# Loading the projection weights without waiting for x, and the output bias row before the first norm

## The chip, the cores and the metric

One Trainium2 chip, one core. The metric is the device time of one launch in microseconds (us). The kernel before takes 1614.23 us (median of 3 runs, 1613.65 to 1616.16). All intermediate work is float32, with matrix products done as three products of float32r (a reduced-precision float32 form for the tensor engine) high and low parts.

## The reference

One encoder layer on 512 tokens of width 1024: RMSNorm, a mixer (a gated depthwise convolution beside a neighbourhood attention, both fed by one input projection), a residual, RMSNorm, a top-4-of-32 mixture of experts, a residual and a last RMSNorm.

```python
def mixer(xn, w_in, b_in, conv_w, conv_b, ln_g, ln_b, rpb, w_out, b_out):
    proj = jnp.einsum("bsd,de->bse", xn, w_in) + b_in          # 1024 -> 2560
    glu_a, glu_g, q, k, v = jnp.split(proj, [...], axis=-1)    # five parts of 512
    conv_out = conformer_conv(glu_a, glu_g, conv_w, conv_b, ln_g, ln_b)   # 31 taps
    na_out = neighbourhood_attention(q, k, v, rpb)
    mixed = jnp.concatenate([conv_out, na_out], axis=-1)
    return jnp.einsum("bse,ed->bsd", mixed, w_out) + b_out

def reference(x, ...):
    h = x
    h = h + mixer(rmsnorm(h, g_mix[0]), ...)
    h = h + moe(rmsnorm(h, g_ffn[0]), ...)      # 32 experts, 3 matrices of 1024 x 1024 each
    return rmsnorm(h, g_final)
```

## The kernel before

Each engine has its own program, written out by hand; semaphores alone order them. There is no planner: what stands in the code is the order of each engine.

Stage 1, the first norm. The 512 tokens are four tiles of 128. SP issues four transfers of x, one per tile, into `h` (L400), then the two small ones of `b_in` and `conv_w` (L401, L402) into a staging area. ACT issues the row of `g_mix`, spread to all partitions (L641), and three small vectors (L644). For each tile ACT squares it and sums (L663), POOL computes 1/rms in two short operations (L514, L516), and DVE scales the tile into `xn_tile` (L939; both inputs, `h` and the `g_mix` row, lie in SBUF). PE turns the tile in eight transposes (L1306); behind those of tile 0 it also turns the staged columns (L1311, L1313), for which it waits for all five small transfers. ACT and DVE copy the turned tile out of PSUM as its high part (L649, L944), and DVE subtracts to get the low part (L949, one input in PSUM).

Stage 2, the input projection. `w_in` comes as five blocks of 512 columns, 2 MB each, into five units of `ring`; SP issues them in the order 1, 0, 2, 3, 4 (L408). Ahead of that SP waits until all four x tiles have landed (L405, L406). A block is used in four groups of 128 columns (the last one in row groups). For each group ACT makes the high part (L677), and the low part is made by DVE for groups 0 to 7 (L961) and by POOL for 8 to 19 (L530); the subtraction reads two SBUF operands. PE runs 24 matmuls per group (L1320, L1321, L1322). Group g needs its low part and a free PSUM bank.

Between the two, POOL adds the row `b_out`, again spread to all partitions (`bout_row`), to each tile of `h` (L525). It waits for that row's transfer, and for tile n until DVE has made `xn_tile` of it (`xn_ready`). ACT issues that transfer (L666) after its last copy of stage 1. The sum is used only much later.

Stage 3. The gate (L969) writes the convolution's input, and the 31 taps run on DVE alone (L978, L986, 4 x 31 instructions). POOL meanwhile builds the attention's bias tables (L544), whose raw rows SP loads pair by pair of heads (L428), each pair after the tables of the one before. Behind these loads on SP stand the two transfers of `w_out` (L433, L435). Then come layer norm of the convolution, attention, output projection, routing and the 32 experts, whose weights stream through SP's queue.

Behind the `w_in` loads SP also issues an 8 MB write of zeros to `y_rows` (L412) and the 16 copies of the position bias (L418).

Of the kernel before, what the change touches and what calls it, by code (L numbers as in the profile page):

```python
# [15 lines left out]
SEQ, D_MODEL = 512, 1024  # L16
GRID_W, N_ROWS = 64, 8
QB = 16
NQ = GRID_W // QB
# [37 lines left out]
def encoder_kernel(nc, x, g_mix, w_in, b_in, conv_w, conv_b, ln_g, ln_b, rpb, w_out, b_out,  # L57
# [3 lines left out]
    with ctx:  # L61
        def sem(name):
            return ctx.enter_context(nc.semaphore(name))
# [52 lines left out]
        def unit(s):  # L116
            return ring[:, s, :].rearrange("p (k f) -> p k f", k=KD)
# [39 lines left out]
        bout_row = area_k[:, 1024:2048]  # L157
# [87 lines left out]
        x_loaded = [sem(f"x_loaded{n}") for n in range(NQ)]  # L245
# [4 lines left out]
        bout_loaded = sem("bout_loaded")  # L250
# [109 lines left out]
        def row_bcast(ap, n, offset=0):  # L360
            return bass.AP(ap.tensor, ap.offset + offset, [[0, P], [1, n]])
# [9 lines left out]
        def piece_src(i, e):  # L371
            return w_rows[i // 4][e, :, (i % 4) * PIECE:(i % 4 + 1) * PIECE]
# [24 lines left out]
        @block.sync  # L397
        def _(sp):
            for n in range(NQ):
                sp.dma_start(h[:, n, :], x_blocks[n]).then_inc(x_loaded[n], 16)  # L400
            sp.dma_start(stage[0:20, 0, :], b_in[0].rearrange("(c p) -> c p", p=P)).then_inc(stage_loaded, 16)  # L401
            sp.dma_start(stage[0:CONV_K * CC, 1, :],  # L402
                         conv_w[0].rearrange("k (c p) -> (k c) p", p=P)).then_inc(stage_loaded, 16)

            for n in range(NQ):  # L405
                sp.wait_ge(x_loaded[n], 16)  # L406
            for i, col in enumerate((1, 0, 2, 3, 4)):
                sp.dma_start(unit(1 + i), win_v[:, :, col * HALF:(col + 1) * HALF]).then_inc(win_loaded[i], 16)  # L408

            spare = y_rows[N_EXPERTS * CAP:, :].rearrange("(p i) (j f) -> p (i j) f", p=CAP, f=HALF)  # L410
            sp.wait_ge(zeros_ready, 1)
            sp.dma_start(spare, zeros[0:CAP].unsqueeze(1).to_broadcast([CAP, spare.shape[1], spare.shape[2]])).then_inc(y_stored, 16)  # L412

            sp.wait_ge(rpb_tile_loaded, 16)
            for c in range(QB):
                sp.dma_start(rpb_pad[c], rpb_tile[:, :]).then_inc(rpb_stored, 16)  # L418
            sp.wait_ge(rpb_stored, 16 * QB)
            copy_size = (HEADS * RPB_H + 1) * RPB_PITCH  # L420
            for pair in range(HEADS // 2):
                if pair:
                    sp.wait_ge(tables_ready, 6 * pair)
                for r in range(N_ROWS):
                    start = (2 * pair * RPB_H + WIN_H - 1 - r) * RPB_PITCH + QB - 1
                    src = bass.AP(rpb_pad.tensor, rpb_pad.offset + start,
                                  [[copy_size - 1, QB], [RPB_H * RPB_PITCH, 2], [1, RUN]])
                    sp.dma_start(raw_bias[r * QB:(r + 1) * QB, :, :], src).then_inc(raw_loaded, 16)  # L428
            def load(i, e):
                sp.dma_start(w_raw[i][:, :], piece_src(i, e)).then_inc(raw_piece[i], 16)  # L430

            sp.wait_ge(proj_done, 12)
            sp.dma_start(unit(1), wout_v[:, :, HALF:]).then_inc(wout_loaded[1], 16)  # L433
            sp.wait_ge(proj_done, 20)
            sp.dma_start(unit(6), wout_v[:, :, 0:HALF]).then_inc(wout_loaded[0], 16)  # L435
            for i in range(3):
                load(i, 0)
            sp.wait_ge(wout_done, 2 * NQ)
            for i in (3, 4):
                load(i, 0)  # L440
            sp.wait_ge(xn2_stored, 16 * NQ)
            load(5, 0)
            load(6, 0)
            sp.wait_ge(bias_rows_loaded, 128)
            for i in range(7, 10):
                load(i, 0)
            sp.wait_ge(overflow_ready, 2)
            sp.wait_ge(xg_loaded, 16)
            load(10, 0)
            sp.wait_ge(xn2_transposed, 2 * NQ)  # L450
            load(11, 0)

            def reload(i, e, at):
                sp.wait_ge(piece_used, at + 1)
                load(i, e)

            for i in range(GATE, DOWN):
                reload(i, 1, i)
            with sp.Fori(0, N_EXPERTS - 2) as j:
                for i in range(DOWN):  # L460
                    reload(i, j + 2, PIECES * j + 8 + i)
                for i in range(DOWN, PIECES):
                    reload(i, j + 1, PIECES * j + 8 + i)
            for i in range(DOWN, PIECES):
                reload(i, N_EXPERTS - 1, PIECES * (N_EXPERTS - 2) + 8 + i)
            trips = sp.value_load(n_ovf[0:1, 0:1], min_val=0, max_val=MAX_OVERFLOW)
            with sp.If(trips > 0):
                with sp.Fori(0, trips) as t:
                    e = sp.value_load(ovf_exp[0:1, bass.ds(t, 1)], min_val=0, max_val=N_EXPERTS - 1)
                    for i in range(PIECES):  # L470
                        reload(i, e, EXTRA_BASE - PIECES + PIECES * t + i)
            for n in range(NQ):
                sp.wait_ge(final_ready, n + 1)
                sp.dma_start(out_blocks[n], y_tok[:, n * TOP_K, :]).then_inc(out_stored, 16)
            sp.wait_ge(out_stored, 16 * NQ)
# [163 lines left out]
        def _(act):  # L639
# [3 lines left out]
            for i, vec in enumerate((conv_b, ln_g, ln_b)):  # L643
                act.dma_start(stage[20 + CC * i:20 + CC * (i + 1), 0, :],  # L644
                              vec[0].rearrange("(c p) -> c p", p=P)).then_inc(stage_loaded, 16)
            def xnT_half(n):

                act.wait_ge(xn_transposed, 2 * n + 2)
                s.copy(xnT_high[:, 4:8, n * P:(n + 1) * P],  # L649
                       bank[4 + (2 * n + 1) % 4][:, :].rearrange("p (k t) -> p k t", k=4)).then_inc(xnT_act, 1)  # L650
# [12 lines left out]
                s.activation(junk_norm[n % 2], h[:, n, :], ACT.Square, accum_out=ss[:, n:n + 1]).then_inc(ss_ready, 1)  # L663
            for n in range(NQ):
                xnT_half(n)
            act.dma_start(bout_row, row_bcast(b_out, D_MODEL)).then_inc(bout_loaded, 16)  # L666
            def win_high_part(g):
                loaded, high, _ = split_parts(g)
                act.wait_ge(win_loaded[4 if g >= 16 else groups[g][0] - 1], 16)

                if 4 <= g < 8:
                    act.wait_ge(proj_done, g - 3)
                elif 9 <= g < 16:
                    act.wait_ge(proj_done, 8)
                elif g >= 16:
                    act.wait_ge(proj_done, 12)
                s.copy(high, loaded).then_inc(win_high_ready, 1)  # L677
# [52 lines left out]
            for i in range(NS):  # L730
                n, hd = steps[i]
# [562 lines left out]
        def _(pe):  # L1294
# [30 lines left out]
            for g in range(16):  # L1325
                if g < 8:
                    pe.wait_ge(win_low_dve, g + 1)
                else:
                    pe.wait_ge(win_low_pool, g - 7)

                if 4 <= g < 12 and g % 2:
                    pe.wait_ge(glu_ready, 4 * ((g - 4) // 2 + 1))
                elif 4 <= g < 12:
                    pe.wait_ge(act_evac, (g - 4) // 2 + 1)
                elif g >= 12:
                    pe.wait_ge(act_evac, 4 + g - 12 + 1)
                _, high, low = split_parts(g)
                for k in range(KD):
                    last = three_products(bank[g % 4][:, :], high[:, k, :], low[:, k, :], xnT_high[:, k, :], xnT_low[:, k, :], k)
                last.then_inc(proj_done, 1)  # L1340
# [245 lines left out]
```

## Time and profile before

| | before |
|---|---|
| median of 3 runs | 1614.23 us |
| profiled execution, its own time | 1613.65 us |
| span of that execution's trace | 1611.9 us |
| PE busy | 1438.2 us (89%) |
| DVE busy | 1293.6 us (80%) |
| ACT busy | 951.7 us (59%) |
| POOL busy | 272.7 us (17%) |
| DMA moved | 476.44 MB, mean 296 GB/s |

The span is cut into engines' busy time; a busy share is an average over stages. The 32 experts fill about the last 1280 us, and PE is busy there nearly throughout. The change lies in the first 60 us, so the rows below are mostly of that stretch. Start times are in us from the start of the span. A matmul's end is modelled, and spans on POOL are rough; the distance between starts is more to be trusted there.

### The profile page before, as it was taken

The page shows a single profiled execution, that of the slowest core. Times are in us where ns is not written, and L with a number is a line of the kernel's source. Part 1 is how long each engine was busy: PE and PEld are TensorE (multiplying, and loading weights), DVE is VectorE, ACT ScalarE, POOL GpSimd, SP SyncE. Part 2 cuts the span into 40 slices and gives each one's busy share as a digit, 9 for nine tenths or more (in the row PEclk, how much of TensorE's full clock was granted, in tenths as well). Part 3 has the DMA queues.
Part 4 walks back from the last instruction along what each step waited for, and adds up shares of the span by engine and source line. Part 5 has one row for each costly group of instructions (what it writes and reads, how often), then busy time and mean ns, then how long its engine had stood idle before and what let it go on. Part 6 is the DMA issues. An engine that isn't in the chain of part 4 may idle for free.

```text
span 1611.9 us, 19217 instructions
## 1 busy us (share of the span) xinstructions
PE 1438.2 (89%) x6488; PEld 1094.5 (68%) x6488; DVE 1293.6 (80%) x933; ACT 951.7 (59%) x708; POOL 272.7 (17%) x287
## 2 busy tenths in 40 slices
PE   4995389956999999999999999999999999999950
PEld 3884157744777777777777777777777777777730
DVE  6899444275888888888888888888888888888836
ACT  2230153233677777777777777777777777777621
POOL 3297730041000000000000000000000000000004
PEclk9998569966999999999999999999999999999985
DMA  7800400075899999999999999999999999999436
GB/s 248 314 10 26 178 17 1 30 261 184 320 363 371 381 376 374 371 376 367 372 370 373 374 374 376 376 373 375 363 371 366 365 395 375 370 373 377 154 140 244
DMA packets 84049, 476.44 MB, mean 296 GB/s; under 512 B 10716, under 2 KB 11015, under 8 KB 34871
## 3 DMA queue, kind: packets, MB, share of 16 engines
q1 hardware_dynamic: 71518, 432.48, 70.5%
q0 software_dynamic: 6560, 23.55, 4.4%
q10 hardware_dynamic: 5944, 20.08, 3.3%
q8 instruction: 15, 0.25, 0.1%
q14 instruction: 12, 0.09, 0.0%
HBM read 448.44 MB, written 27.63 MB: 295 GB/s over the span
## 4 chain that ended last, share of the span: by engine, by line
PE 83%; POOL 5%; DVE 5%; DMA 3%; ACT 1%; issue 1%; SPq 1%; POOLq 0%; DVEq 0%; ACTq 0%
PE pair L1498 22%; PE pair L1497 22%; PE pair L1496 22%; PE pair L1503 3%; POOL area_t L544 3%; PE pair L1320 2%; PE pair L1321 2%; PE pair L1322 2%; PE pair L1476 2%; PE pair L1483 1%; DVE h L1284 1%; PE pair L1362 1%; DMA area_m<-in_conv_w 1%; PE pair L1381 1%; POOL ring L544 1%
## 5 line engine op out<-in xcount | busy, mean ns | idle before, releaser
L1124 DVE TENSOR_TENSOR w_low<-w_raw,w_high 128x2048 fp32r<-128x2048 f32 x381 | 867.3, 2291 | 142.5 <-ACT w_high L794 142.4
L794 ACT CAST w_high<-w_raw 128x2048 fp32r<-128x2048 f32 x384 | 734.2, 1913 | 323.3 <-PE pair L1498 314.9
L1498 PE MATMUL pair<-w_high,xT_low 128*112 128x512 f32 x1024 | 405.2, 396 | 0.0
L1496 PE MATMUL pair<-w_high,xT_high 128*112 128x512 f32 x1024 | 404.9, 395 | 0.0
L1497 PE MATMUL pair<-w_low,xT_high 128*112 128x512 f32 x1024 | 404.9, 395 | 0.0
L1497 PEld LDWEIGHTS pair<-w_low,xT_high 128*112 128x112 f32 x1024 | 179.6, 175 | 58.1
L1496 PEld LDWEIGHTS pair<-w_high,xT_high 128*112 128x112 f32 x1024 | 179.8, 176 | 57.3
L1498 PEld LDWEIGHTS pair<-w_high,xT_low 128*112 128x112 f32 x1024 | 179.5, 175 | 57.0
L1496 PE MATMUL pair<-w_high,hT_high 128*112 128x512 f32 x512 | 202.3, 395 | 0.0
L1498 PE MATMUL pair<-w_high,hT_low 128*112 128x512 f32 x512 | 202.2, 395 | 0.0
L1497 PE MATMUL pair<-w_low,hT_high 128*112 128x512 f32 x512 | 201.3, 393 | 0.0
L591 POOL CAST sel_gate<-is_expert 128x112 fp32r (+1 forms) x32 | 32.5, 1014 | 656.7 <-PE pair L1498 656.7
L1497 PEld LDWEIGHTS pair<-w_low,hT_high 128*112 128x112 f32 x512 | 89.6, 175 | 30.1
L1498 PEld LDWEIGHTS pair<-w_high,hT_low 128*112 128x112 f32 x512 | 89.6, 175 | 29.4
L1496 PEld LDWEIGHTS pair<-w_high,hT_high 128*112 128x112 f32 x512 | 89.3, 174 | 28.7
L986 DVE SCALAR_TENSOR_TENSOR area_m<-area_u,convT,area_m 128x512 f32<-128x512 f32 x120 | 108.0, 976 | 0.0
L595 POOL CAST sel_down<-is_expert 128x112 fp32r (+1 forms) x32 | 9.2, 287 | 366.3 <-PE pair L1498 366.3
L1232 DVE SCALAR_TENSOR_TENSOR area_q<-area_t,area_q 112x1024 f32<-112x1024 f32 x32 | 65.3, 2041 | 0.0
L737 ACT ACTIVATE area_a<-area_a,area_u 128x256 f32<-128x256 f32 (+1 forms) x32 | 18.0, 561 | 57.6 <-DVE area_u L1023 57.6
L1322 PE MATMUL pair<-xnT_high,win_low 128*128 128x512 f32 x128 | 50.8, 397 | 0.0
L544 POOL TENSOR_TENSOR area_t<-area_m 128x384 f32<-128x384 f32 x8 | 46.5, 5808 | 16.2 <-DMA area_m<-rpb_pad 16.2
L843 ACT CAST xT_high<-pair 128x896 fp32r<-128x896 f32 x33 | 29.6, 898 | 25.9 <-PE pair L1476 25.9
(246 smaller groups left out, 1422.4 us busy)
## 6 DMA issues: line engine op xcount, KB each, us to landing
w_raw<-in_w_gate SPq DMA_DIRECT2D x128, 1024.0 KB, 6.9
w_raw<-in_w_up SPq DMA_DIRECT2D x128, 1024.0 KB, 6.7
w_raw<-in_w_down SPq DMA_DIRECT2D x128, 1024.0 KB, 6.8
y_rows<-area_m ACTq DMA_DIRECT2D x32, 448.0 KB, 5.5
ring<-in_w_in SPq DMA_DIRECT2D x5, 2048.0 KB, 19.1
y_rows<-area_t SPq DMA_DIRECT2D x1, 8064.0 KB, 37.7
ring<-in_w_out SPq DMA_DIRECT2D x2, 2048.0 KB, 10.4
h<-in_x SPq DMA_DIRECT2D x4, 512.0 KB
```

Source lines behind the costliest of these rows:

```text
L544: g.tensor_tensor(dst.rearrange("p (m r c) -> p m r c", r=N_ROWS, c=QB), src, mask[:, o:o + w].rearrange("p (m r c) -> p m r c", r=N_ROWS, ...
L591: g.tensor_copy(sel_gate[:, :], is_expert[:, bass.ds(e, 1)].to_broadcast([P, CAP]))
L794: s.copy(w_high[:, i % HIGH_RING, :], w_raw[i][:, :]).then_inc(high_ready, 1)
L986: v.scalar_tensor_tensor(mixedT[:, c, :], u_pad[:, c, bass.ds(k, SEQ)], convT[:, bass.ds(k * CC + c, 1)], mixedT[:, c, :], ALU.mult, ALU.a ...
L1124: v.tensor_tensor(w_low[i][:, :], w_raw[i][:, :], w_high[:, i % HIGH_RING, :].bitcast(F32), ALU.subtract).then_inc(low_ready, 1)
L1232: v.scalar_tensor_tensor(h_tok.rearrange("q (k p) -> q p k", k=KD), g_silu.rearrange("q (p k) -> q p k", k=KD), SILU_TOP, u_lim.rearrange( ...
L1320: t.matmul(to, a_high, b_high, start=(k == 0), stop=False)
L1322: return t.matmul(to, a_low, b_high, start=False, stop=(k == KD - 1))
L1496: t.matmul(to[half], tok_high, hi, start=False, stop=False)
L1497: t.matmul(to[half], tok_high, lo, start=False, stop=False)
L1498: last = t.matmul(to[half], tok_low, hi, start=False, stop=(k == KD - 1))
L1503: t.matmul(to[half], sel[:, :], rows[:, half * HALF:(half + 1) * HALF], start=True, stop=False)
```

## The change

Two edits. SP no longer waits for the four x tiles before it issues the five loads of `w_in`. And the transfer of the `b_out` row, which ACT issued after its four copies of the first norm, is issued directly behind the three small vectors, before the first square.

```diff
@@ SP
             sp.dma_start(stage[0:CONV_K * CC, 1, :],
                          conv_w[0].rearrange("k (c p) -> (k c) p", p=P)).then_inc(stage_loaded, 16)
 
-            for n in range(NQ):
-                sp.wait_ge(x_loaded[n], 16)
             for i, col in enumerate((1, 0, 2, 3, 4)):
                 sp.dma_start(unit(1 + i), win_v[:, :, col * HALF:(col + 1) * HALF]).then_inc(win_loaded[i], 16)
@@ ACT
             for i, vec in enumerate((conv_b, ln_g, ln_b)):
                 act.dma_start(stage[20 + CC * i:20 + CC * (i + 1), 0, :],
                               vec[0].rearrange("(c p) -> c p", p=P)).then_inc(stage_loaded, 16)
+            act.dma_start(bout_row, row_bcast(b_out, D_MODEL)).then_inc(bout_loaded, 16)
+
@@
             for n in range(NQ):
                 xnT_half(n)
-            act.dma_start(bout_row, row_bcast(b_out, D_MODEL)).then_inc(bout_loaded, 16)
```

On ACT the order of the first instructions was this (area_k holds the two rows, area_t takes the squares, xnT_high is the high part of the turned tile, glu_high that of the weights):

```order
L644 DMA area_m<-in_conv_b 4x128
L644 DMA area_m<-in_ln_g 4x128
L644 DMA area_m<-in_ln_b 4x128
L663 ACT_TABLE_LOAD
L663 ACTIVATE area_t,ss<-h 128x1024 [waits x_loaded0]
L663 ACTIVATE area_t,ss<-h 128x1024 [waits ss_ready,x_loaded1]
L663 ACTIVATE area_t,ss<-h 128x1024 [waits ss_ready,x_loaded2]
L663 ACTIVATE area_t,ss<-h 128x1024 [waits ss_ready,x_loaded3]
L649 CAST xnT_high<-pair 128x4x128 [waits xn_transposed] x4
L666 DMA area_k<-in_b_out 128x1024
L677 CAST glu_high<-ring 128x1024 [waits win_loaded0]
```

In the changed kernel it is this:

```order
L642 DMA area_m<-in_conv_b 4x128
L642 DMA area_m<-in_ln_g 4x128
L642 DMA area_m<-in_ln_b 4x128
L644 DMA area_k<-in_b_out 128x1024
L663 ACT_TABLE_LOAD
L663 ACTIVATE area_t,ss<-h 128x1024 [waits x_loaded0]
L663 ACTIVATE area_t,ss<-h 128x1024 [waits ss_ready,x_loaded1]
L663 ACTIVATE area_t,ss<-h 128x1024 [waits ss_ready,x_loaded2]
L663 ACTIVATE area_t,ss<-h 128x1024 [waits ss_ready,x_loaded3]
L649 CAST xnT_high<-pair 128x4x128 [waits xn_transposed] x4
L676 CAST glu_high<-ring 128x1024 [waits win_loaded0]
```

One DMA instruction moved past the squares and the copies. On SP no instruction moved, only the waits on x are gone; PE, DVE and POOL have the same instructions in the same order.

## Rows read from the trace of the kernel before

**Rows 1.** Chain of waits, 0 to 60 us: start us, us, what.
```profile
5.08 15.30 DMA area_m<-in_conv_w
...
21.14 0.87 PE pair L1306 x4
22.01 1.28 DVE area_q L939
...
30.73 1.14 DVE win_low L961
32.01 0.77 PE pair L1320
...
37.47 0.42 PE pair L1320
37.88 0.23 PE pair L1321
```

**Rows 2.** Chain of waits, 140 to 230 us.
```profile
142.76 33.12 POOL area_t L544
...
183.18 7.91 DMA ring<-in_w_out
```

**Rows 3.** Who waits, PE, 32 to 141 us: us in total, times, longest.
```profile
PE pair L1320 <- DVE win_low L961: 3.6, 1, 3.6
```

**Rows 4.** Timeline of DVE: start us, us, line, operation, count [idle before, releaser].
```profile
22.00 1.28 DVE L939 SCALAR_TENSOR_TENSOR area_q<-h,rstd,area_k 128x1024 f32<-128x1024 f32 x1
23.20 0.68 DVE L944 CAST xnT_high<-pair 128x512 fp32r<-128x512 f32 x1
...
25.12 1.28 DVE L939 SCALAR_TENSOR_TENSOR area_q<-h,rstd,area_k 128x1024 f32<-128x1024 f32 x1
...
30.64 1.22 DVE L961 TENSOR_TENSOR win_low<-ring,glu_high 128x1024 fp32r<-128x1024 f32 x1
35.48 10.13 DVE L961 TENSOR_TENSOR win_low<-ring,glu_high 128x1024 fp32r<-128x1024 f32 x3 [3.62 <-ACT glu_high L677]
45.96 1.13 DVE L969 SCALAR_TENSOR_TENSOR area_u<-pair,colT,area_v 128x128 f32<-128x128 f32 x4 [0.34 <-PE pair L1322]
...
56.78 1.13 DVE L969 SCALAR_TENSOR_TENSOR area_u<-pair,colT,area_v 128x128 f32<-128x128 f32 x4 [6.68 <-PE pair L1322]
```

**Rows 5.** Timeline of POOL, 20 to 66 us.
```profile
21.25 0.55 POOL L516 TENSOR_TENSOR rstd<-ms,small 128x1 f32<-128x1 f32 x1
35.47 12.42 POOL L525 TENSOR_TENSOR h<-h,area_k 128x1024 f32<-128x1024 f32 x4 [13.66 <-DMA area_k<-in_b_out]
```

**Rows 6.** POOL's additions at L525: duration ns min/median/max, first and last start.
```profile
L525 POOL TENSOR_TENSOR h<-h,area_k x4: 2383/3385/3392, 35.5 to 44.5; 128x1024 f32<-128x1024 f32 x4
```

**Rows 7.** Timeline of ACT, 0 to 40 us.
```profile
3.24 1.28 ACT L663 ACT_TABLE_LOAD   x1 [3.24 <-issue]
9.31 1.06 ACT L663 ACTIVATE area_t<-h 128x1024 f32<-128x1024 f32 x1 [4.79 <-DMA h<-in_x]
...
19.74 1.06 ACT L663 ACTIVATE area_t<-h 128x1024 f32<-128x1024 f32 x1 [2.14 <-DMA h<-in_x]
...
28.94 1.05 ACT L677 CAST glu_high<-ring 128x1024 fp32r<-128x1024 f32 x1
34.40 2.94 ACT L677 CAST glu_high<-ring 128x1024 fp32r<-128x1024 f32 x3 [4.42 <-DMA ring<-in_w_in]
```

**Rows 8.** DMA queues, 0 to 6 us: packets, MB, share of 16 engines.
```profile
q10 hardware_dynamic: 152, 0.53, 38.2%
```

**Rows 9.** DMA queues, 10 to 18 us.
```profile
q1 hardware_dynamic: 323, 1.22, 50.4%
```

**Rows 10.** DMA queues, 28 to 36 us.
```profile
q1 hardware_dynamic: 1288, 2.61, 88.2%
q10 hardware_dynamic: 144, 0.52, 16.8%
```

**Rows 11.** Timeline of SP, 0 to 31 us.
```profile
5.08 0.27 SPq L402 DMA_DIRECT2D area_m<-in_conv_w  x1
19.80 16.52 SPq L408 DMA_DIRECT2D ring<-in_w_in  x5
```

**Rows 12.** Busy time by stretch: PE, PEld, DVE, ACT, POOL (instructions), clock, DMA share, GB/s.
```profile
60.00:131.00 71.00, 71.00 (x315) 58.80 (x314) 71.00 (x72) 17.98 (x22) 45.67 (x19) 1.00 0.26 82
```

## The prediction

> **What bounds the kernel now.** I read the chain of waits first, for the stretch that the change touches. It begins with the x transfers' queue: the small transfer of `conv_w` is issued at 5.08 and lands at 20.38, then come PE's transposes, then DVE work without a break, and PE's first projection matmul starts at 32.01 [rows 1]. Next I read who PE waits for between 32 and 141 us: only that one wait of 3.6 us, for DVE's first low part, and none after it [rows 3]. So from 32.01 on the projection is PE at its own pace. DVE, in turn, idles 6.68 us for PE ahead of the gate at 56.78 [rows 4], and is then busy for the whole of 60 to 131 us [rows 12]. POOL's table at 142.76 ends only when the taps do, and the `w_out` load at 183.18 hangs behind it [rows 2]. Hence the reader is to see one chain: PE's first projection matmul, group 3 of the projection, the gate, the taps, the tables, `w_out`, and everything behind. There is no slack on it between 32 us and the end, so a shift of PE's start is a shift of the end, microsecond for microsecond. The whole question is when that first matmul starts.
>
> What does it wait for? The first weight block does not appear: ACT takes its group 0 at 28.94 without waiting for a transfer. ACT waits 4.42 us for the second block, until 34.40 [rows 7]. The low part of group 1 is made from 35.48 and is ready about 3.4 us later, near 38.9 (three such operations take 10.13 us) [rows 4]. PE needs it after the 24 matmuls of group 0: about 13 of 0.43 us and 11 of 0.23 us from 32.01 [rows 1], so near 40.2. It is there 1.3 us early. So neither weight block is late for PE now.
>
> **SP's removed wait.** SP could issue `w_in` at 5.4 instead of 19.8 [rows 11]. What it buys is small. While x runs, queue 1 keeps 50.4% of 16 engines busy [rows 9], which I read as eight engines full and eight idle: 323 packets in 8 us x 16 x 0.504 = 64.5 us of engine time are 0.20 us for a 4 KB packet, no slower per byte than the 2 KB packets of the weights (8 x 16 x 0.882 = 113 us over 1288, 0.088 us each) [rows 10]. On the eight idle engines the weights' halves start early; on the eight that carry x they stand behind x in the same queue and end when they end now, plus what x is late. So the first block still lands around 28 to 30 us, and PE did not wait for it. Value 0. Its bounds: at best, if a weight wait were hidden in PE's slow start, the 13 matmuls would run at 0.23 instead of 0.43 us, a gain of 2.6 us; at worst the loads take packets from x (rival 3).
>
> The Trainium skill (page "DMA: Bandwidth & Descriptors", section "Why a DMA increments its semaphore by 16 and not by 1", and its summary row on using all 16 engines) has a copy run on as many engines as its slowest dimension allows; the x tile's slowest source dimension is 8 grid rows. The 50.4% agrees with eight.
>
> **The moved `b_out` transfer, on the queue.** 128 rows of 4 KB, 0.52 MB, on ACT's queue 10, and all 16 engines take part. Now it runs in 28 to 36 us beside the weights; there it costs nothing that PE waits for. In the changed kernel it follows `g_mix` directly and runs into x. Its issue (0.4 us or so) is before the table load at 3.24 and ACT idles 4.79 us before x lands at 9.31 [rows 7], so ACT loses nothing. But each of the eight full engines must also carry eight of its packets. Their price: in 0 to 6 us queue 10, which is `g_mix`, took 38.2% of 6 us, 2.3 us per engine, or (6 x 16 x 0.382)/152 = 0.24 us a packet, 1.9 us for eight [rows 8]. In 28 to 36 us queue 10 took 16.8% of 8 us, 1.3 us per engine [rows 10]. I take 1.9, the row of the same stage beside the same x transfers; bounds 1.3 and 2.3, and 0 if the engines have gaps (rival 2). Since x is back to back (landings at about 9.3 and 19.7 [rows 7]), all of it lands later by that, `conv_w` behind it too, and with both the chain of rows 1. **+1.9 us.**
>
> **The moved `b_out` transfer, on POOL.** POOL's four additions waited for this row until 35.47 [rows 5], when DVE's urgent part was over. Now the row is there early, and POOL starts as soon as its last 1/rms is done: 21.25 + 0.55 = 21.80 in the old times. That is the middle of the DVE run 22.00 to 31.9 that starts PE. The trace shows what they do to each other: three low parts that take 1.22 us alone took 10.13 us beside the additions, 3.4 each [rows 4], and an addition takes 3.39 beside them [rows 6], so they take turns; less DVE's 1.15 an addition holds for 2.2 us. The gate at 45.96, which reads PSUM and one SBUF operand, took the same 1.13 us beside POOL as at 56.78 without it [rows 4]. So of DVE's run only the operations with two SBUF inputs are hit: tile scalings 2 and 3 (L939) and the first low part (L961).
>
> The Trainium skill ("SBUF — State Buffer", on the port pair that DVE and GpSimd share) says the pair is an exclusive lock for a whole instruction, taken by DVE when both of its inputs are in SBUF; it would make the scaling wait like the subtraction. The 3.4 us agree for the subtraction; no row shows the scaling beside POOL.
>
> Played through in the old times (add 1.9 to all): addition 0 from 21.80 to 24.0. Scaling 2 wanted 22.00, gets 24.0: 2.0 late. Addition 1 from 25.2 to 27.4. Scaling 3 comes 3.12 us after scaling 2 (22.00 to 25.12), so wants 27.1, gets 27.4: 2.3 late. Addition 2 from 28.6 to 30.8, addition 3 to 33.0. The low part comes 5.52 us after scaling 3 (25.12 to 30.64), wants 32.9, gets 33.0: 2.4 late. **+2.4 us** on PE's start. The additions end near 33 instead of 47.9, and DVE's later low parts run at 1.2 us, which PE doesn't need. Bounds: 0 if the scaling isn't hit and the low part slips between; 6.6 if each of the three operations waits for a whole addition (3 x 2.2).
>
> **Sum.** 1.9 + 2.4 = +4.3 us. Against the profiled execution's own 1613.65 that is 1617.95; the median shown is 0.58 higher, so I forecast 1618.5.
>
> **Rivals.**
> 1. Not slower: DVE wins the race at 22 us. POOL is ahead by 0.2 us only (21.80 against 22.00), and POOL's spans are rough. Then scaling 2 is on time, addition 0 runs 23.2 to 25.4, scaling 3 is 0.3 late, additions 1 and 2 run 26.6 to 31.0, and the low part wants 30.9: 0.4 in all. With 1.9 for the queue 2.3 us: 1616.5. The point that decides is whether the first addition starts before scaling 2. For it: the small margin. Against: both hang on the same square of tile 3, so the margin moves with them.
> 2. The engines that carry x are half idle each instead of eight being full; then `b_out` fits in. Only the port's 2.4 us remain: 1616.6. Against it the packets' own 0.20 us.
> 3. The weights take packets from x. If they alternate from 6 us on, the remaining 1.7 MB of x go at half of 153 GB/s (1.22 MB in 8 us): 11 us later, with the port 13: 1627. Against it: the four x tiles and `conv_w`, all issued by 5.4, land one behind the other on this queue. A mild form, x's engines slowed by the others being busy, would be 2 to 4 us more, 1621.
> 4. Faster: the earlier weights and a DVE free of POOL after 35 us reach PE in a way the waits don't show. At most the 2.6 us above and no loss: 1611.6.
>
> **How the numbers follow.** A measurement of this kernel tells about 0.2%, 3.2 us, from no change. Forecast 0.50, rival 1 0.17, rival 2 0.10, rival 3 0.14 with its mild form, rival 4 0.09. Rivals 1 and 2 fall within 0.2%, and so does about a fifth of the forecast: its own sum runs from 3.7 (1.3 + 2.4) to 4.7 us (2.3 + 2.4), and the runs shown spread over 2.5 us. Slower 0.53, same 0.38, faster 0.09. The range takes in rivals 1 and 2 and the mild form of 3: 1614.5 to 1622.5; the forecast's own is 1617 to 1620.
>
> **What would show it.** Right: the first square at about 11.2 instead of 9.31 and the last at 21.6 instead of 19.74; `conv_w` landing near 22.3; additions at L525 from about 23.7, ending near 35; scaling 2 lasting or starting over 2 us later than a shift of 1.9 explains; PE's first matmul near 36.3; no further change of distance between that matmul, the gate and the taps. Wrong: x landing as before (queue term), L939 at 1.28 us without an added gap (port term), x landing beyond 24 us (rival 3), or a distance from the first matmul to the end of the taps that has changed by over 1 us, which would break the chain on which the sum rests.

## The result, and the profile after

The changed kernel takes 1623.7 us (median of 4 runs, 1619.36 to 1626.43) beside 1614.43 for the one before in the same session: 0.53% slower, 95% interval 0.30% to 0.78%. The direction was forecast, the size was not: 1618.5 with a range up to 1622.5. The profiled execution is one of the quicker ones, 1620.81 us with a span of 1619.0, so it shows 7.1 us of loss and not the median's 9.

The chain of waits of the changed kernel, 0 to 60 us (start us, us, what), answers [rows 1]:

```profile
3.03 24.72 DMA h<-in_x
27.77 1.15 ACT area_t L663 x2
...
41.08 1.14 DVE win_low L960
42.35 0.76 PE pair L1319
```

PE's first projection matmul starts at 42.35 instead of 32.01: 10.34 us late. The chain now begins with x itself. The last tile's square at 27.77 is also past the 24 us that the prediction named as the sign of its rival 3. ACT's timeline, 0 to 45 us, answers [rows 7]:

```profile
10.48 1.06 ACT L663 ACTIVATE area_t<-h 128x1024 f32<-128x1024 f32 x1 [5.39 <-DMA h<-in_x]
...
16.18 1.06 ACT L663 ACTIVATE area_t<-h 128x1024 f32<-128x1024 f32 x1 [4.55 <-DMA h<-in_x]
...
21.92 1.06 ACT L663 ACTIVATE area_t<-h 128x1024 f32<-128x1024 f32 x1 [4.59 <-DMA h<-in_x]
...
27.77 1.06 ACT L663 ACTIVATE area_t<-h 128x1024 f32<-128x1024 f32 x1 [4.71 <-DMA h<-in_x]
...
39.06 3.88 ACT L676 CAST glu_high<-ring 128x1024 fp32r<-128x1024 f32 x4
```

The tiles come 5.7 to 5.9 us apart, where they came 3.5 apart before (9.31 to 19.74 over three steps), and the last square is 8.0 us late. The weights, on the other hand, are all there when ACT turns to them at 39.06: its 4.42 us of waiting for the second block are gone, and bought nothing. DVE and POOL in the same stretch answer [rows 4, 5]:

```profile
30.03 3.19 DVE L938 SCALAR_TENSOR_TENSOR area_q<-h,rstd,area_k 128x1024 f32<-128x1024 f32 x1
...
35.06 1.46 DVE L938 SCALAR_TENSOR_TENSOR area_q<-h,rstd,area_k 128x1024 f32<-128x1024 f32 x1
...
40.99 4.62 DVE L960 TENSOR_TENSOR win_low<-ring,glu_high 128x1024 fp32r<-128x1024 f32 x4
```

```profile
29.28 0.55 POOL L514 TENSOR_TENSOR rstd<-ms,small 128x1 f32<-128x1 f32 x1
29.80 11.25 POOL L523 TENSOR_TENSOR h<-h,area_k 128x1024 f32<-128x1024 f32 x4
```

POOL's first addition starts at 29.80, 0.23 us ahead of scaling 2 at 30.03, and that scaling lasts 3.19 us instead of 1.28. From its start to the first matmul it is 12.32 us, before 10.01. So 10.34 = 8.03 (x late) + 2.31 (DVE held by POOL's additions, called the port term below). Of the 2.31, 1.91 lie in scaling 2, 0.18 in scaling 3 (1.46 instead of 1.28) and 0.21 in a small operation of DVE on four columns (0.38 instead of 0.17); the first low part takes 1.14 us on the chain, as before.

What the DMA engines did: queues of the changed kernel, 18 to 24 us, when x and the weights ran together, answering [rows 9, 10] (packets, MB, share of 16 engines; queue 1 is SP's, queue 10 ACT's):

```profile
DMA packets 406, 1.08 MB, mean 179 GB/s; under 512 B 16, under 2 KB 16, under 8 KB 406
...
q1 hardware_dynamic: 406, 1.08, 104.9%
```

All 16 engines are busy, and yet they move 179 GB/s, hardly more than the 153 of x alone on eight, and less than half of the 391 of the weights and b_out together (2.61 + 0.52 MB in 8 us, [rows 10]). Sorting the trace's packets of queue 1 by size tells whose time went where (mean us per packet; the run with the wait alone removed comes in the next section):

```
                                      x, 4 KB    w_in, 2 KB
before, x alone, 10 to 18 us          0.22       -
before, w_in alone, 22 to 30 us       -          0.087
changed, both, 14 to 26 us            0.37       0.20
wait alone removed, both, 10 to 26    0.40       0.22
changed, w_in alone, 30 to 36 us      -          0.090
```

From 18 to 24 us, 135 packets of x at 0.36 us and 255 of the weights at 0.20 us make 8.1 and 8.6 of them under way at a time. So x does stay on eight engines and the weights on the other eight, and each half moves about 90 GB/s, where x alone moved 152.

### The profile page after: what moved, and what is told of

It is laid out like the page before. It is cut to its first block, busy times and chain, and to the rows that moved or that the text cites. A ratio compares the mean times of both kernels' runs of the same rounds, so it can differ in the third digit from the quotient of the medians.

```text
span 1619.0 us, 19215 instructions
## 1 busy us (share of the span) xinstructions
PE 1433.7 (89%) x6488; PEld 1094.3 (68%) x6488; DVE 1288.5 (80%) x933; ACT 951.3 (59%) x708; POOL 271.2 (17%) x287
## 4 chain that ended last, share of the span: by engine, by line
PE 83%; POOL 6%; DVE 4%; DMA 3%; ACT 1%; issue 1%; SPq 1%; POOLq 0%; ACTq 0%
PE pair L1497 22%; PE pair L1496 22%; PE pair L1495 22%; PE pair L1502 3%; POOL area_t L542 3%; PE pair L1319 2%; PE pair L1320 2%; PE pair L1321 2%; PE pair L1475 2%; DMA h<-in_x 2%; PE pair L1482 1%; PE pair L1361 1%; POOL ring L629 1%; PE pair L1380 1%; POOL ring L542 1%
## 5 line engine op out<-in xcount | busy, mean ns | idle before, releaser
L736 ACT ACTIVATE area_a<-area_a,area_u 128x256 f32<-128x256 f32 (+1 forms) x32 | 18.0, 561 | 56.2 <-DVE area_u L1022 56.1
```

## The experiments

All ratios are against the kernel before on the same chip, with the 95% interval in brackets. Start times are from one profiled execution each, and x's landing differs between executions, so a difference of 1 or 2 us between two profiles is not shown by them alone.

**One edit at a time.** The removed wait alone (the two lines of SP's wait taken out, b_out late as before):

> Only SP's wait on x is removed; the b_out row keeps its late place. Theory now: the weights' packets on the eight engines that x leaves free slow x's own packets (in the changed kernel 4 KB packets of x went from about 0.22 to 0.36 us), so the x tiles land about 5.8 us apart instead of 3.5; last square near 26 instead of 19.74, PE's first projection matmul near 38.5 (before 32.01), no port collision, and the kernel is 5 to 6 us slower than before. Rival, the recorded prediction: the removed wait is worth nothing, last square at 19.7, first matmul at 32, time within 1 us of before. Rival 2: x is slowed only by the three-way mix with b_out, then the last square is near 21.

1.0045 (1.0032 to 1.0058). Its x, ACT's timeline, 0 to 40 us:

```profile
9.55 1.06 ACT L661 ACTIVATE area_t<-h 128x1024 f32<-128x1024 f32 x1 [5.09 <-DMA h<-in_x]
...
28.00 1.06 ACT L661 ACTIVATE area_t<-h 128x1024 f32<-128x1024 f32 x1 [5.00 <-DMA h<-in_x]
```

Four tiles 6.1 us apart, the first matmul at 40.26, and no b_out near. In time it is 7.3 us (5.2 to 9.4). The prediction's value of 0 for this edit falls, and so does rival 2 of this run, that it takes b_out as well: the weights alone do it.

The moved b_out alone, wait kept; and the same with `pool.wait_ge(win_high_ready, 2)` ahead of POOL's additions, which puts them back where they were:

> Only the b_out transfer is moved forward; SP's wait stays. Theory: queue term 1.3 to 2.3 us (last square near 21.6 instead of 19.74) plus 2.0 to 2.4 us of port collision in front of PE's first matmul (near 36.1), in all 3 to 4 us slower, part of it given back later by PE's clock. Rival: b_out costs x nothing without the weights (last square at 19.7) and only the collision is left, 2 us.

> As the kernel with only b_out moved forward, but POOL's four additions of it also wait until ACT has made the second group of weights' high part, where they ran before. The port collision goes, the queue term stays: theory 1.5 to 2 us faster than with b_out moved alone, first matmul near 34; the scalings of tiles 2 and 3 at 1.28 us. If the collision is not what delays PE, the two kernels are equal.

1.0030 (1.0019 to 1.0040) and 1.0012 (1.0001 to 1.0023). Their difference, 0.18% or 2.9 us (2.1 by the two medians), is the port term. In the profile of b_out alone scaling 2 again takes 3.19 us, and from it to the first matmul it is 12.33 us (22.71 to 35.04); with the additions late it is 10.01 (25.32 to 35.33). What is left with the additions late, 0.12% or 1.9 us, is the queue term. The two programs have the same transfers up to there, yet their last squares were at 20.45 and 23.06: x's landing scatters from one execution to the next, so the queue term is known from the timed runs only, and to about 1.8 us either way.

The additions late in the changed kernel, both edits in:

> The changed kernel, but POOL's additions wait for the second group's high part, so they run where they ran before. Theory: takes away the port collision of about 2 to 3 us, leaves the late x: 0.3 to 0.4% slower than before, last square near 27.8, first matmul near 40 instead of 42.35. Rival: with x so late the collision costs nothing; then equal to the changed kernel's 0.53%.

1.0057 (1.0043 to 1.0070), beside 1.0053 for the change. The profile shows the collision gone (31.06 to 41.07 is 10.01 us again), but x came 1.0 us later still (last square 28.79), and the times show no gain. This profile was 9.25 us behind the one before at the convolution's low part and only 5.6 at the end, so what happens behind the 60 us that the change touches is as large as the term looked for. Whether the port is worth its 2.3 us in this kernel's time is not settled by these intervals.

A part of the wait: the first weight block ahead of the wait on x, the other four behind it.

> The kernel before, but the first of the five weight loads is issued ahead of the wait on x, the other four behind it. Eight idle engines carry 1 MB of it beside x. Theory (side by side, each stream at about 90 GB/s): it slows x for about 11 us, so two tiles land 5.8 us apart and two 3.5; last square near 24, kernel 3 to 4 us slower. Rival: the loss needs all five loads in the queue; then under 1 us.

1.0029 (1.0016 to 1.0041), 4.7 us. The profile, of its quickest run, has the last square at 21.43, only 1.7 us late; its packets of x took 0.30 us beside the weights' 0.16 (10 to 18 us), quicker than in the run with the wait alone removed. By the times one block in the queue costs about 0.6 of what all five cost, though the intervals are wide.

**Why x is slow, and slower with company.** My reading was eight engines full and eight idle, and that x is slow because it has only eight. First all 16: x by grid row, `h[r*16:(r+1)*16, :, :]`, eight transfers of 16 tokens by four tiles.

> The kernel before (wait kept, b_out late), but x is loaded by grid row, eight transfers of 16 tokens by four tiles each, so that the slowest dimension is 16 and all 16 engines take part; all tiles share one semaphore. Theory that the four tile transfers use eight engines only: 2 MB land in 6 to 8 us of streaming, the first square near 10 and the last near 13.5 (before 19.74), the weights follow at once, PE's first matmul near 24 to 26, the kernel 5 to 8 us faster. Rival: x is slow for its 4 KB rows or for its place in memory, not for the number of engines; then all squares come after 19 us and the kernel is 3 us slower.

1.0034 (1.0022 to 1.0046). Its queues from 10 to 18 us:

```profile
DMA packets 356, 1.08 MB, mean 135 GB/s; under 512 B 81, under 2 KB 96, under 8 KB 356
...
q1 hardware_dynamic: 324, 1.07, 102.5%
```

All engines busy and x no faster: 135 GB/s, the first square at 20.55. So more engines alone do not make x faster. Next the source in 128 consecutive rows, with SP's wait and without it. This changes three things at once: the source's pieces, the number of engines (queue 1 at 88.9% of 16 in 5 to 9 us) and which partitions are written together. It reads the tokens in another order, so it serves as an experiment only.

```diff
-                sp.dma_start(h[:, n, :], x_blocks[n]).then_inc(x_loaded[n], 16)
+                sp.dma_start(h[:, n, :], x[0, n * P:(n + 1) * P, :]).then_inc(x_loaded[n], 16)
```

> The kernel before (wait kept, b_out late), but each x tile is read as 128 consecutive rows instead of 8 pieces of 16 rows; the tokens stand in another order, so the output is that of permuted tokens. The source's slowest dimension is now 128. Theory after the run by grid rows (where 16 engines took 0.48 us a packet and x still moved about 150 GB/s): what limits x is its pattern, source pieces or destination partitions in step, not the number of engines; then the flat tiles land about 1.5 us apart, last square near 13.5 instead of 19.74, and the kernel is 5 us or more faster. Rival: x is limited by where it lies in memory or by the first 20 us of the launch; then the flat tiles still land about 3.5 us apart and nothing changes.

> As the flat x, and SP does not wait for x. If the weights slow x only because x's pattern is slow and leaves engines to them, the flat x lands as with the wait (within 1 us) and the missing wait costs nothing or gains up to 2 us. If a later transfer of the same queue takes bandwidth from an earlier one in any case, the last square is later than with the wait by 2 us or more.

0.9952 (0.9937 to 0.9967) and 0.9956 (0.9941 to 0.9972). ACT's timeline with the wait (first and last tile), then without it (last tile):

```profile
6.24 1.06 ACT L663 ACTIVATE area_t<-h 128x1024 f32<-128x1024 f32 x1 [2.33 <-DMA h<-in_x]
...
10.35 1.06 ACT L663 ACTIVATE area_t<-h 128x1024 f32<-128x1024 f32 x1 [0.21 <-DMA h<-in_x]
```

```profile
10.49 1.06 ACT L661 ACTIVATE area_t<-h 128x1024 f32<-128x1024 f32 x1 [0.19 <-DMA h<-in_x]
```

The tiles are 1.4 us apart instead of 3.5, and now the removed wait costs x 0.14 us. Here x uses all 16 engines, and the first packet of the weights starts at 9.40, when x is all but through (10.02). The weights do not overtake x in the queue.

Source or destination? Eight source pieces of 16 rows, 17 rows apart instead of 64, the same destination:

> The kernel before, but the eight source pieces of an x tile lie 17 rows apart instead of 64 (it reads other tokens, so the output is not the reference's); eight pieces of 16 rows, eight engines and the destination stay. Theory: x is slow for where it is written (eight engines that write partitions 16 apart in step, so few of SBUF's write ports at a time); then tiles still land about 3.5 us apart and the time is that of before. Rival: x is slow because its source pieces are a large power of two apart in memory; then the tiles land under 2.5 us apart and the kernel is 3 us or more faster.

0.9998 (0.9985 to 1.0010), tiles 3.8 us apart. The distance in memory is not it. Then the order of the rows: those of the run by rows, dealt over SP's and ACT's queues in two ways. In the first, ACT has rows 5, 4, 7, 6; in the second, SP has rows 0, 1, 4, 5 and ACT 2, 3, 6, 7. What differs is which groups of 16 partitions are written at a time, and with them which rows of the source are read at a time. SP's edit of the first, against the run by rows:

```diff
-            for r in range(N_ROWS):
+            for r in (0, 1, 2, 3):
                 sp.dma_start(h[r * QB:(r + 1) * QB, :, :], x_rows[r]).then_inc(x_loaded[0], 16)
```

> x by grid row as in the run by rows (16 engines, 0.48 us a packet, last row landed near 20.5), wait kept, b_out late, but the eight row transfers go out on two queues: SP's for rows 0 to 3, ACT's for rows 5, 4, 7, 6, ahead of g_mix. Two groups of partitions are then written at a time, chosen so that they share no port by the write-side theory. Theory: about twice the rate, first square near 11 to 13 instead of 20.55, PE's first matmul near 29, kernel 1 to 3 us faster than before. Rival: the queue or the source limits x at 150 GB/s; first square again near 20, kernel 3 us or more slower.

> As the two queues with the wait, but the rows are dealt out so that the two queues write the same group of ports: SP 0, 1, 4, 5 and ACT 2, 3, 6, 7. Theory of the ports: slower than the other deal, first square 4 us or more later, near 17 to 20. Rival: only the second queue matters; then both deals land x alike within 1 us.

1.0008 (0.9996 to 1.0019) and 1.0036 (1.0023 to 1.0048). ACT's first square in the one and the other:

```profile
15.72 1.06 ACT L666 ACTIVATE area_t<-h 128x1024 f32<-128x1024 f32 x1 [9.96 <-DMA h<-in_x]
```

```profile
20.59 1.06 ACT L666 ACTIVATE area_t<-h 128x1024 f32<-128x1024 f32 x1 [14.79 <-DMA h<-in_x]
```

Sizes, count and queues are alike, and so is what is copied; the order alone moves x by 4.9 us in the profiles, and the time by 0.28%, 4.5 us. A second queue by itself brings nothing: the second deal is where the run by rows on one queue was (20.55, 1.0034). The Trainium skill ("SBUF — State Buffer", section "Door 1: The DMA port swizzle") has DMA bandwidth depend on how many of 16 write ports the partitions reach, partitions 32 apart sharing one, and this is how the two deals were chosen; they agree with it. That makes the write side the likely limit, with the run at another source distance beside it, but it is not isolated: each row has its fixed place on both sides, so no run changes the order of writing without that of reading. The Trainium skill ("DMA: Bandwidth & Descriptors", section "Back-pressure in remote DMA") says of transfers between cores that a saturated destination port stalls the engines that share its path. Here the transfers are from memory, and no run shows at which port, or whether at one, the weights' packets waited.

The better deal without SP's wait:

> As the two queues, and SP does not wait for x before the weights. Theory: x keeps the engines busy now and is early, so the weights cost it 0 to 2 us; equal to the two queues with the wait within 0.2%. Rival: x is still slow on its ports and the weights beside it slow it as in the changed kernel: first square 4 us or more later than with the wait.

1.0006 (0.9997 to 1.0014), first square at 16.15: the wait costs nothing here either. And here x is slow: its packets took 0.37 to 0.41 us (8 to 14 us). What sets this run apart from the changed kernel is that x leaves no engines to the weights, whose first packet starts at 12.75 instead of 8.23 with the wait alone removed.

**Looking for a version that beats both.** Each tile as eight row transfers, dealt over both queues so that neighbours write different groups (SP rows 0, 5, 3, 6; ACT 4, 1, 7, 2); the same without the wait; and that with b_out ahead of the squares, where it stands behind all of x:

> x tile by tile again, but each tile as eight row transfers, dealt over SP's queue (rows 0, 5, 3, 6) and ACT's (4, 1, 7, 2, with g_mix behind tile 0), one packet per engine and transfer, so that neighbouring packets go to different groups of partitions. Wait kept, b_out late; each tile's semaphore waits for all eight. Theory (the write side limits x): all four tiles are there by 11 to 13 us, last square near 13 to 15 instead of 19.74, PE's first matmul near 26 to 28 instead of 32.01, kernel 4 to 6 us faster than before. Rival: many small transfers cost what they bring (issue 0.42 us each, 16 per queue, and ACT issues before it squares): last square after 18 us, no gain.

> As the dealt rows, without SP's wait on x. Theory: x keeps all 16 engines, so the weights queue behind it: squares within 1 us of those with the wait, time equal within 0.2% or up to 1 us faster. Rival: weights slow x whatever its pattern; squares 3 us or more later.

> As the dealt rows without the wait, and b_out is issued behind the small vectors, which here is behind all of x. Theory: no queue term, only POOL's additions in DVE's run before the first matmul: 2 to 3 us slower than the dealt rows without the wait, scaling 2 at 3.2 us instead of 1.28. Rival: the collision is harmless when x is early; equal.

1.0005 (0.9996 to 1.0015), 1.0002 (0.9991 to 1.0012) and 1.0016 (1.0006 to 1.0025). The expectation of 4 to 6 us failed: the last squares were at 19.72, 17.02 and 19.87, and x's packets still took 0.37 to 0.51 us (8 to 14 us). The rival, the cost of issuing, is not it either: in the first of the three the last transfer of x was issued by 8.9 us, and the squares of tiles 2 and 3 waited 3.00 and 1.72 us for data. A deal made to spread the writes did not speed x up, which speaks against the write side as the whole reason; why these packets stay slow is open. As in the two queues, the missing wait did no harm (the weights' first packet at 14.73). So no order of x that keeps the tokens in place and that I ran beats the kernel before; the flat one does, by 7.7 us, but reads another order of tokens. The third run has b_out behind x and agrees with the port term: 0.14% or 2.2 us over the second, though the two intervals just overlap, and scaling 2 at 3.18 us.

## Why the prediction was wrong

**SP's removed wait, valued at 0.** This is the step that failed. It said that eight engines were full, that packets of x cost no more per byte than those of the weights, and that the weights on the idle eight would therefore run beside x for free, while behind x they would "end when they end now". Eight and eight was right, and so was the queue order. The inference from idle engines to free bandwidth was not: with both halves at work a packet of x took 0.40 us instead of 0.22 and one of the weights 0.22 instead of 0.09, and x moved 82 GB/s instead of 152. Measured: 0.45%, 7.3 us, by itself. A part of the inference was a misreading even of the rows: 0.20 us for 4 KB is 0.10 for 2 KB against 0.088, and the 0.20 is an average with small packets in it. The 4 KB packets alone took 0.22, a quarter more per byte than the weights, and 0.16 in the flat order, so x was already slowed by something. It was rival 3 at 0.14, whose full form (11 us) and mild form (2 to 4) lay on either side of the 8.0 us that x lost. The halved rate of the full form came, but from about 10 us on and by the weights on the other engines; on x's own engines they did not alternate with it. What the two halves compete for is open.

**b_out on the queue, +1.9.** 1.9 us in the timed runs (0.12%, from 0.2 to 3.7). Together with the port term b_out alone cost 4.8 us (3.1 to 6.5), where the prediction's sum was 4.3. Whether the term is still there beside the weights is not settled: x's last square was as late with the wait removed alone (28.00) as with both edits (27.77), while the two edits' 0.45% and 0.30% add up to 0.75%, which the interval of the change (0.30% to 0.78%) still holds.

**b_out on POOL, +2.4.** Right in place and size: 2.31 us in the changed kernel's profile, 2.3 in the other, 2.9 and 2.2 in two timed differences; the third, in the changed kernel itself, shows none. The race was won by POOL by 0.23 us, forecast 0.2; rival 1 did not occur in the three profiles where the additions were early. That a scaling with two SBUF inputs is held like the subtraction, which no row of before showed, is shown by its 3.19 us.

That the change came out slower was forecast for reasons that explain less than half of it. The weights alone would have made it slower without either term of the sum, so the right direction is in part luck.

**No slack on the chain, microsecond for microsecond.** Held to the end of the taps, 132.98 + 42.05 = 175.03 before and 143.50 + 42.04 = 185.54 after, 10.5 us later, and to the load of `w_out` (183.18 and 193.69). Then it gave way: ACT reaches the step behind the layer norm's variance (L737, L736) 9.2 us later, and the attention's step on DVE at L1019 (209.36 and 217.25) and the low part of the convolution (229.09 and 236.96) 7.9 us later. The matmuls for the variance, before and after (groups by line), lie on the chain:

```profile
L1421 PE MATMUL pair<-area_u,mean_w 128*128 128x512 f32 x8 | 6.6, 1003 | 13.2 <-ACT area_u L723 13.2
```

```profile
L1420 PE MATMUL pair<-area_u,mean_w 128*128 128x512 f32 x8 | 5.3, 811 | 14.7 <-ACT area_u L722 14.7
```

More of them ran at 2.4 GHz instead of 1.2: the granted clock was 0.59 of full speed in 195 to 203 us before and 0.75 in 205 to 213 after. The edits do not bring it: with the additions late in the changed kernel they took 1008 ns and with the wait alone removed 989, and the latter carried its loss through, 8.25 us at the first matmul, 8.0 at the convolution's low part, 8.5 in the span (1620.4). The kernel before is one of the slow cases of this. From the first projection matmul to the convolution's low part it took 197.1 us, with b_out alone 196.9, but 193.2 with the additions late besides and 193.7 with one block ahead, so this stretch alone moves a profile by up to 4 us, nearly as much as the whole forecast. A part of the spread of 7 us among the changed kernel's runs may be this and x's scattered landing; that was not tested run by run.

## What to carry to other kernels

Idle DMA engines are not free bandwidth: a later load on the eight engines that x left idle halved x's rate, while in the three cases where x had all 16 engines the later load stayed behind it and cost nothing, whether x was fast or slow. So before letting a load loose beside a critical one, ask how many engines the critical one leaves. A wait that looks like lost time can be what keeps the critical load alone; test it by removing it alone. And a row that arrives earlier starts its consumer earlier: look at what that consumer shares with the engine on the chain.

## What the runs showed that I had not expected

- A load that keeps all 16 engines busy can move 135 GB/s or 399 GB/s of the same array into the same tile, by the rows read and the partitions written at a time (x by rows, 10 to 18 us, against x flat, 5 to 9 us; flat reads the tokens in another order):

```profile
DMA packets 476, 1.60 MB, mean 399 GB/s; under 512 B 76, under 2 KB 88, under 8 KB 476
```

- Two deals of the same eight transfers over two queues differ by 4.9 us in landing 2 MB, and by 4.5 us in the kernel's time.
- The slowed company loses more than the slow load: 2 KB packets of the weights went from 0.087 to 0.20 us, x's 4 KB from 0.22 to 0.37.
